# First half of the in-chunk matrices loaded before the last two pool spreads, and the pool matrix scaled before the last two gates of the state-space branch

## The reference, cut to what matters

```
h = rms_norm(x, norm1); z = h @ w_in
y_a = s5_mixer(z[:512])         # complex state-space scan, 32 groups of 64 states, gelu, gate
y_b = conv_module(z[512:1536])  # a * sigmoid(b), causal depthwise conv of 31 taps, LayerNorm, silu
y_c = pool_mixer(z[1536:2048])  # causal means over 2, 4, 8, 16 steps minus the input
p = einsum('bsgc,gcd->bsgd', p, w_group) * scale ; y_c = p @ w_proj
x = x + (g0 * y_a + g1 * y_b + g2 * y_c) @ w_out   # g = sigmoid(z[2048:] + b_gate)
x = x + (silu(h2 @ w_gate) * (h2 @ w_up)) @ w_down
```

## Time and profile before

| what | value |
|---|---|
| median of 3 runs | 2078.76 us (2078.09 to 2083.53) |
| the profiled execution's own time | 2079.5 us |
| its span, slowest core (core 4) | 2077.9 us |
| spans of the 8 cores | 2075.7, 2075.1, 2069.8, 2076.2, 2077.9, 2071.8, 2073.3, 2076.8 us |
| mean granted TensorE clock | 0.986 to 0.990 |
| TensorE busy | 1983.5 us, 95% |
| DVE, ACT, POOL busy | 1005.4, 675.9, 87.2 us |
| share of TensorE in the chain that ended last | 87% |

### The profile page before, as it was taken

The page is one execution under the profiler, slowest core; times in us unless marked ns, Lnnn a source line. Parts: engine busy times, 40 slices in busy tenths (PEclk is TensorE's granted clock), DMA queues, the critical chain, the costliest instruction groups (busy, mean ns, idle before and its releaser), DMA issues.

```text
span 2077.9 us, 31140 instructions; the slowest of 8 cores (2069.8 to 2077.9 us)
## 1 busy us (share of the span) xinstructions
PE 1983.5 (95%) x11536; PEld 919.7 (44%) x11536; DVE 1005.4 (48%) x1480; ACT 675.9 (33%) x1122; POOL 87.2 (4%) x164
## 2 busy tenths in 40 slices
PE   3799899999999999999999989999999999999996
PEld 1344544444444444444444454444444444444443
DVE  6789564444454444433353875544436223133135
ACT  6633682222333203115242258322224110111123
POOL 1001000000000000000000000000000000000000
PEclk9899999999999999999999999999999999999998
DMA  9537242112422313135378644212142220412103
GB/s 238 122 66 138 52 102 42 33 29 41 142 51 46 67 17 69 32 67 97 86 195 164 137 84 82 70 33 41 31 139 55 41 39 3 71 31 51 31 11 162
DMA packets 57235, 156.31 MB, mean 75 GB/s; under 512 B 6016, under 2 KB 26880, under 8 KB 54528
## 3 DMA queue, kind: packets, MB, share of 16 engines
q0 software_dynamic: 22032, 79.14, 22.8%
q1 hardware_dynamic: 32176, 72.03, 11.7%
q10 hardware_dynamic: 2880, 3.15, 0.6%
HBM read 193.58 MB, written 25.17 MB: 105 GB/s over the span
## 4 chain that ended last, share of the span: by engine, by line
PE 87%; ACT 4%; DVE 3%; issue 2%; DMA 2%; SPq 0%; DVEq 0%; ACTq 0%
PE ps L254 87%; DMA km<-k_mid 1%; DMA uc<-stg 1%; ACT yb L243 1%; ACT sq_s L243 1%; DVE cv L224 1%; ACT po L243 0%; DVE h L232 0%; SPq L270 0%; DVE gt L224 0%; ACT ph L243 0%; ACT L243 0%; ACT ps L243 0%; ACT g L243 0%; DVE idx L228 0%
## 5 line engine op out<-in xcount | busy, mean ns | idle before, releaser
L254 PE MATMUL ps<-h,slot 128*128 128x512 bf16 x5376 | 1203.9, 380 | 8.7 <-DVE h L232 6.6
L254 PEld LDWEIGHTS ps<-h,slot 128*128 128x128 bf16 x5376 | 525.4, 98 | 643.4 <-issue 19.1
L224 DVE TENSOR_TENSOR actb<-ps,sgf 128x512 bf16<-128x512 f32 x176 | 121.5, 691 | 419.5 <-PE ps L254 400.2
L254 PE MATMUL ps<-actb,slot 128*128 128x512 bf16 x1408 | 305.9, 379 | 0.0
L243 ACT ACTIVATE sgf<-ps 128x512 f32<-128x512 f32 x176 | 105.1, 597 | 595.2 <-PE ps L254 585.6
L232 DVE SCALAR_TENSOR_TENSOR acc<-gt,ps 128x512 f32<-128x512 f32 x180 | 123.4, 687 | 238.9 <-PE ps L254 236.7
L243 ACT ACTIVATE gt<-ps,hb 128x512 f32<-128x512 f32 x192 | 130.8, 686 | 331.4 <-PE ps L254 331.2
L254 PEld LDWEIGHTS ps<-actb,slot 128*128 128x128 bf16 x1408 | 137.6, 98 | 165.9 <-issue 0.2
L224 DVE TENSOR_TENSOR x<-ps,x 128x512 f32<-128x512 f32 x192 | 130.2, 689 | 134.6 <-PE ps L254 134.6
L261 POOL DMA_DIRECT2D slot<-wts x150 | 79.3, 532 | 1826.8 <-PE ps L254 1788.0
L254 PE MATMUL ps<-mg,slot 128*128 128x512 bf16 x512 | 114.9, 386 | 5.8 <-DVE mg L232 5.8
(11 more groups left out here) (130 smaller groups left out, 1197.7 us busy)
## 6 DMA issues: line engine op xcount, KB each, us to landing
slot<-wts POOLq DMA_DIRECT2D x150, 512.0 KB, 6.9
x<-xT SPq DMA_DIRECT2D x16, 512.0 KB, 18.1
x<-xT SPq DMA_DIRECT2D x4, 2048.0 KB, 16.0
x_mid<-x SPq DMA_DIRECT2D x4, 2048.0 KB, 8.9
x<-x_mid SPq DMA_DIRECT2D x4, 2048.0 KB, 18.0
outT<-x SPq DMA_DIRECT2D x4, 2048.0 KB, 6.4
uc<-stg SPq DMA_DIRECT2D x64, 64.0 KB, 6.6
hc<-stg SPq DMA_DIRECT2D x32, 128.0 KB, 2.9
```

The costliest lines, as they stand in the source:

```text
L224: return (eng or dve).put(lambda e: e.tensor_tensor(out=out, in0=a, in1=b, op=op), after)
L254: ins = e.matmul(out, lhsT=a, rhs=b, start=start and i == 0, stop=stop and i == n - 1, **kw)
```

## The change

In both layers the first half of KM is loaded before pool blocks 2 and 3 are projected, the second half where both were. For this, pool block 2 is staged in a new seventh tile, STG[6], at offset 40960 (over TG[0], TG[1] and LT[0]); pool block 3 stays in tile 3. Block 2's evictions now wait for the TG tiles to be read instead of for the landing of conv block 2's spread, the first half of KM waits for that landing, and writers of LT wait for STG[6]'s spread. Separately, the load of WGRF and the 4 scalings into WGS leave `fold` and stand ahead of `glu(2)` as `fold_scale`. The numbers of tiles and semaphores follow.

```diff
-    STG = [... enumerate((0, 4096, 32768, 36864, 8192, 12288))]
+    STG = [... enumerate((0, 4096, 32768, 36864, 8192, 12288, 40960))]
 def p_blk(b):
-            k = 4 + b if b < 2 else b
-            after = S["x2_free" if k in (2, 3) else "x0_free"]
+            k = (4, 5, 6, 3)[b]
+            after = S["x0_free"] if b < 2 else S["x2_free"] + (S["tg_free"] if k == 6 else [])
 def ln_sum(b):
-            S["la_free"] = tt(LT[b % 2][:, 1], ..., [ta, S["tmp_free"]] + S["tg_free"] + S["lt_free"][b % 2])
+            S["la_free"] = tt(LT[b % 2][:, 1], ..., [ta, S["tmp_free"]] + S["tg_free"] + S["stg_free"][6] + S["lt_free"][b % 2])
 def ln_stat(b):
-            te = actv(mu, ps[:, i], AF.Identity, [t_mu, S["tmp_free"]] + S["tg_free"] + S["lt_free"][b % 2])
+            te = actv(mu, ps[:, i], AF.Identity, [t_mu, S["tmp_free"]] + S["tg_free"] + S["stg_free"][6] + S["lt_free"][b % 2])
+        def fold_scale():
+            t_g = dma(sp, WGRF[:, :], d_wgrp[l], d_wgr, S["tg_free"])
+            S["wgs"] = [actv(WGS[:, g], WGRF[:, g], AF.Copy, [t_g, t_cols, S["pool_pe"]], scale=col(c_psc + g)) for g in range(4)]
         def fold(ws):
-            t_g = dma(sp, WGRF[:, :], d_wgrp[l], d_wgr, S["tg_free"])
-            tg = [actv(WGS[:, g], WGRF[:, g], AF.Copy, [t_g, t_cols, S["pool_pe"]], scale=col(c_psc + g)) for g in range(4)]
+            tg = S["wgs"]
+        def km_load(h):
+            q = slice(8 * h, 8 * h + 8)
+            S["km"].append(dma(sp, KM[:, q], s_k[:, q], d_kl[h], S["x2_free"] + out["k"] + S["stg_free"][2 + h]))
 # both layers
+            km_load(0)
             S["ws_p"] = [slot(l, "p", c) for c in range(2)]
             for _ in some_of(p_blk, (2, 3)):
...
-        for h in range(2):
-            q = slice(8 * h, 8 * h + 8)
-            S["km"].append(dma(sp, KM[:, q], s_k[:, q], d_kl[h], S["x2_free"] + out["k"] + S["stg_free"][2 + h]))
+        km_load(1)
...
         ln_sum(3)
+        fold_scale()
         glu(2)
         glu(3)
         fold([slot(l, "wpc", h) for h in range(2)])
```

More of the change, by code:

```diff
@@ L182, in build_program @@
     ACCE = [at("acce%d" % i, [3, 512], F32, o_rc + 8192 * i) for i in range(2)]
-    STG = [at("stg%d" % i, [4, 512], BF16, o_x + o) for i, o in enumerate((0, 4096, 32768, 36864, 8192, 12288))]
+    STG = [at("stg%d" % i, [4, 512], BF16, o_x + o) for i, o in enumerate((0, 4096, 32768, 36864, 8192, 12288, 40960))]
     SQ = {k: at("sq_" + k, [8, 512], BF16, o) for k, o in (("rb", o_rb), ("s", o_rc))}
@@ L961, in ln_sum @@
             ta = tt(LA[:, 0:2], cv[:, 0:2], cv[:, 2:4], ALU.add, tc + [S["la_free"], S["tmp_free"]])
-            S["la_free"] = tt(LT[b % 2][:, 1], LA[:, 0], LA[:, 1], ALU.add, [ta, S["tmp_free"]] + S["tg_free"] + S["lt_free"][b % 2])
+            S["la_free"] = tt(LT[b % 2][:, 1], LA[:, 0], LA[:, 1], ALU.add, [ta, S["tmp_free"]] + S["tg_free"] + S["stg_free"][6] + S["lt_free"][b % 2])
             S["la"][b] = S["la_free"]
@@ L1070, in layer @@
                  acc_free=[None] * 2, mg=[[] for _ in range(4)], var=[None] * 4, rs=[None] * 4, ln=[None] * 4)
-        S["stg_free"] = {k: [] for k in range(6)}
+        S["stg_free"] = {k: [] for k in range(7)}
         S["hp_free"], S["rots"] = None, iter(())
@@ L1429, in build_program @@
     d_pt_sem = dsem("pt")
-    d_stg = rot("stg", 6)
+    d_stg = rot("stg", 7)
     spill_sem = rot("spill", 4)
```

## The result

| | before | after |
|---|---|---|
| median of the runs, us | 2078.55 | 2070.45 |
| profiled execution, its own time, us | 2079.5 | 2069.13 |
| mean span of the 8 cores in it, us | 2074.6 | 2066.0 |
| stage from the end of the convolution to `st2(2)`, first layer, mean of 8 cores, us | 31.99 | 24.46 |
| the same, second layer, us | 25.94 | 25.10 |

The kernel is faster by 0.46%: the ratio is 0.9954, with a 95% interval from 0.9941 to 0.9966. The forecast was 2071.3 us. The mean spans differ by 8.6 us, and the stage of the two layers explains 7.5 + 0.8 = 8.3 us of it. (All comparisons leave disturbed runs out.)

The account below looks back on a forecast made before the run. TensorE, holding 87% of the chain, bounds the kernel; time is won where it waits or its clock is low. Gains 6.2 + 1.3 + 0 = 7.5 us from 2079.5 give 2072.0, less 0.74 to the median: 2071.3 us, range 2065.0 to 2076.5.

Parts of the forecast that it names:

- First half of KM, first layer: Before `st2(0)`: the 8.69 us KM wait goes, a fetch stop appears; gain 6.2 us, bounds 4.4 to 9.7.
- First half of KM, second layer: Before `st2(0)`: the 1.52 us wait goes, the stop may lengthen; gain 1.3 us, between 0 and 2.7.
- The spreads: Pool blocks 2 and 3: UC complete 0 to 3.0 us later than 212.72; counted as nothing.
- the slow rival: Block 2's spread waits for the whole early KM load, UC comes last in the first layer; 2084.0 us, chance 0.04.
- `fold_scale`: Fold: the 1.43 us WGS wait goes but the merge starts no earlier; 0 us, bounds -0.3 and +1.43 a layer.
- Staging tile: Block 2's evictions wait for TanH tiles to be read; 0 to 0.5 us on ACT, nothing on TensorE.
- The low clock: First layer, behind the stop in or near `st2(1)`: granted clock of 0.50 for some microseconds.
- The stop as instruction fetch: In `st2`: TensorE's stops without releaser, 1.83 to 3.07 us, are instruction packets coming late beside full DMA engines.
- the long wait did not hide the fetch: First layer, before `st2(0)`: the prediction said the 8.69 us KM wait had hidden instruction fetches.
- was timed by the DMA load, not by TensorE's progress: Second layer's `st2`: of the packet ending the stop; TensorE coming 1.5 us earlier may stand 1.5 us longer.
- The full gain: Rival for both layers' stages: no fetch stop, gain 14.3 us, 2064.5 us; chance 0.18.
- the stop takes the whole of the wait's place: Rival: first layer's stage gains only 1.8 us, the second layer's nothing; 2077.0 us, chance 0.18.

Follow-up runs that it names:

- the extra copies: Two HBM-to-HBM copies of 1 MB each added per layer to the changed kernel, beside the loads of `cd` 7 and `cd` 8; 2086.57 us, ratio 1.0028.

## Why the prediction was right, step by step

*First half of KM, first layer: right.* The load is early, the wait is gone on every core, and a stop appears. The stage was set to 25.4 us from three cores of the other layer and came to 24.46 as a mean, 25.98 on core 4. The gain of 6.2 us is 7.5 as a mean over the cores and 5.7 on core 4, both within 4.4 to 9.7. The runs with the KM part alone and with it left out show that it is this step that pays. The early load left at 180.08 on core 4, not at 185, and took 6.4 us (6.2 to 8.0 over the cores), not the 14.17 that I carried over. The sum came closer than its terms: this step was set 1.3 us too low and the next 0.5 too high.

*First half of KM, second layer: right in sign, uncertain in size.* I took 1.3 us, the middle between 0 and 2.7. The stage's mean fell by 0.8 us, core 4's by 3.25; the run with the early load in the first layer only puts it at 1.5 us by medians, within what runs differ by. That a TensorE that comes earlier may only stand longer is seen on core 1: its KM wait of 4.1 us went, a stop of 2.4 us came where there was none, and its stage stayed as it was, 25.75 and 25.70 us.

*The spreads: the count of nothing held, the bounds did not.* UC was to be complete 0 to 3.0 us later. On core 4 it came 0.2 us earlier, but on core 2 it came at 212.42 instead of 206.6, 5.8 us later, and on core 7 at 209.33 instead of 213.24, 3.9 us earlier. From core to core this time moves by more than the 512 KB that I priced. It cost nothing, as argued: `pool_edge` begins at 214.53, behind the stop. With the extra copies UC did come last, as in the slow rival though for another reason, at the price of 4.6 to 6.1 us.

*`fold_scale`: right.* Nothing, for the reason given: the merge waits for DVE and for its weights. Runs with and without it agree, and so do the means from `glu(3)` to the merge (7.20 and 7.03 us against 7.21 and 7.16).

*Staging tile: right.* Nothing, shown by the run with it alone.

*The low clock: right on half of the cores, not on core 4.* It was to stand at 0.50 for some microseconds right behind the first layer's stop. It does, within about 1 us, on cores 1, 2, 6 and 7, with stops of 3.06, 2.26, 1.99 and 2.06 us. Cores 0 and 3, with 1.70 and 2.79 us, stay at 1.00. Cores 4 and 5, with 2.24 us each, fall only around their second stop. So the length of the stop alone does not tell. Core 7 and then core 3, the stop and the stretch behind it:

```profile
212.20 0.29 PE L254 MATMUL ps<-ud,km 128*32 128x256 bf16 x3 [2.06 <-issue]
213.70:217.00 3.30, 1.39 (x85) 1.30 (x77) 3.30 (x3) 2.18 (x5) 0.00 (x0) 0.50 0.07 25
```

```profile
212.51 0.29 PE L254 MATMUL ps<-ud,km 128*32 128x256 bf16 x3 [2.79 <-issue]
213.70:217.00 3.30, 1.38 (x91) 1.24 (x86) 3.30 (x3) 2.18 (x5) 0.00 (x0) 1.00 0.01 3
```

*The stop as instruction fetch: right, and the packets' times show it.* The stop sits beside full DMA engines, grows with their load (mean 2.3 to 6.2 us) and goes without it, on the same instructions. No record names TensorE's fetch as the releaser, but the packets of the instruction queue q8 can be dated with short windows of the DMA view. Core 4, from 210.8 to 211.8 us in the changed kernel:

```profile
q0 software_dynamic: 35, 0.09, 44.4%
q8 instruction: 1, 0.02, 6.1%
```

from 207.4 to 208.4 us with four loads held:

```profile
q8 instruction: 1, 0.02, 5.5%
```

and from 217.0 to 217.5 us in the kernel before, which has none from 205 to 217:

```profile
q8 instruction: 1, 0.02, 12.1%
```

It is the same packet each time, the tenth of this queue. In the changed kernel it starts at 210.9 us, when TensorE has just run dry (210.84), and takes 0.98 us (6.1% of 16 engines for 1 us); TensorE goes on 1.2 us after its end, at 213.09. This holds everywhere: over all cores of the 14 profiles, the two stages have 143 stops without a releaser of more than 0.8 us, and every one ends 0.85 to 1.62 us (median 1.39) after an instruction packet has ended. Counted from the start of `st2(0)`, the tenth packet of the 8 cores starts after 1.2 to 1.9 us with four loads held, 4.3 to 5.8 us in the changed kernel and 7.4 to 9.6 us with the extra copies. By the Trainium skill ("Runtime: NRT & Kernel Launch", section "Instruction fetch mechanics") this fetch is hidden; the stops of 1.7 to 3.1 us on all cores, and their end when the weights are held, speak against it here.

One detail of the prediction is wrong: the long wait did not hide the fetch. In the kernel before, the tenth packet starts only 1.2 to 3.2 us after TensorE has gone on behind the KM wait, on all 8 cores. So it follows TensorE's progress and then, beside full DMA engines, comes late; the KM wait had put it off to a time when they were emptier (share 0.60 at 213 to 217 us). That the packet "was timed by the DMA load, not by TensorE's progress" is therefore half of it.

*The rivals.* The full gain, 2064.5 us, was ruled out by the stops; the two runs of the changed kernel that take most or all of them away come to 2067.06 and 2065.77, so its price was near, though holding weights changes more than the stops. That the stop takes the whole of the wait's place is ruled out too: as means of the 8 cores it takes 2.3 us of 8.9. The forecast's own case was given as 2068.5 to 2075.5; its gains of 4.4 to 8 and 0 to 2.7 us add up to 2068.1 to 2074.4, which would not have changed the outcome.

*What the prediction did not see* is the cheaper lever. It took the 14 us of a KM load as given and moved its issue; the 14 us were themselves mostly the weights' doing. The fastest kernels here are those with weight loads held: 0.9921 and 0.9926 with the change and four loads, 0.9925 with the change and three, 0.9924 with three and without the change. Their intervals do not tell them apart.

## What to carry to other kernels

When a small load is late, look at what fills the DMA engines before moving its issue: here bulk weight loads that nobody needed yet made the late KM, the late UC and the instruction stops, and holding them back shortened the stage more than the early issue did. When TensorE stands idle with no releaser, date the packets of the instruction queue: here each such stop ended a little over 1 us after one. A longer wait ahead may put the fetch off to a time when the DMA engines are free; so removing that wait can bring a stop that the trace before does not show, and it has to be taken off the gain. A wait taken from one operand pays only if the next operand, here the merge's weights, is not due at the same time.

## What the runs showed of the hardware

The first half of KM, a 512 KB load issued near 200 us, took 11.9 to 15.7 us over the 8 cores beside the weight loads and 5.5 to 6.5 us with three of them held. The same stretch of `st2` stopped for 1.7 to 3.1 us with the DMA engines full, for 5.5 to 7.6 us with 2 MB more to move in each layer, and not at all with four weight loads held on the changed kernel. Each stop of more than 0.8 us ended 0.85 to 1.62 us after the end of an instruction packet, and in the first layer that packet started 1.2 to 1.9, 4.3 to 5.8 or 7.4 to 9.6 us after `st2` had begun, as the DMA load rose. The granted clock stayed at 1.00 behind first-layer stops of 1.70 and 2.79 us and fell to 0.50 within about 1 us of stops of 1.99, 2.06, 2.26 and 3.06 us, on different cores; around core 4's second stop of 2.31 us, which followed a first stop of 2.24 and a wait of 1.92 us, it was 0.52.
